# A fused decoder-layer kernel: where the down-weight differences are loaded and formed, and where S1 of the down-projection is summed

## What is computed

```python
h = x + jnp.concatenate([out_a, out_b, out_c], axis=-1) @ lw['w_o']
h = h + memory_attend(rmsnorm(h, lw['norm_mem_g']), mem_k, mem_v, lw)      # ends in o @ lw['w_mo']
u, ffn_buf_new = causal_dwconv(rmsnorm(h, lw['norm_ffn_g']) @ lw['w_up'], ffn_buf, lw['w_ffn_conv'])
ug, uv = split_cols(u, (D_FF, D_FF))
h = h + (jax.nn.silu(ug) * uv) @ lw['w_down']
```

## Time and profile before

| | us |
|---|---|
| runs shown (three) | 1825.99, 1829.52, 1831.13 |
| median | 1829.52 |
| the profiled execution's own time | 1829.62 |
| its span, first to last instruction | 1828.3 |
| PE busy in it | 1754.7 |
| granted TensorE clock, mean | 0.991 |

### The profile page before, as it was taken

One profiled execution on the slowest core, in us unless ns is written; L12 is line 12 of the kernel. 1 busy time (PEld: TensorE's weight loads), 2 busy tenths in 40 slices (PEclk: granted clock), 3 DMA queues, 4 the chain that ended last, 5 costly groups with the idle time before them and its releaser, 6 DMA issues. The chain is left out here.

```text
span 1828.3 us, 27754 instructions
## 1 busy us (share of the span) xinstructions
PE 1754.7 (96%) x10342; PEld 1603.5 (88%) x10342; DVE 1163.1 (64%) x1381; ACT 781.4 (43%) x1489; POOL 725.6 (40%) x617
## 2 busy tenths in 40 slices
PE   6999999989989989999999989999999999999999
PEld 5999999988867778898788879999999999987887
DVE  6236765865665664422537388888888888657964
ACT  5126773325566332312234265444444444443432
POOL 4001211025444250112116027776666666456642
PEclk9999999999989999999999999999999999999999
DMA  6222111233254274133615522222222222499653
GB/s 174 73 60 62 37 36 50 86 97 111 64 155 166 113 279 139 35 115 124 211 42 208 188 66 73 72 72 72 72 72 72 72 72 72 159 321 304 202 181 128
DMA packets 173568, 215.05 MB, mean 118 GB/s; under 512 B 14695, under 2 KB 122600, under 8 KB 171648
## 3 DMA queue, kind: packets, MB, share of 16 engines
q1 hardware_dynamic: 172560, 213.55, 35.9%
q0 software_dynamic: 896, 0.19, 0.1%
q10 hardware_dynamic: 16, 0.00, 0.0%
HBM read 167.11 MB, written 46.60 MB: 117 GB/s over the span
## 5 line engine op out<-in xcount | busy, mean ns | idle before, releaser
L3904 PE MATMUL ffn_banks<-h_parts,up_hi 128*128 128x384 f32 x1920 | 488.7, 335 | 7.9 <-DVE h_parts L4400 4.5
L3904 PEld LDWEIGHTS ffn_banks<-h_parts,up_hi 128*128 128x128 f32 x1920 | 345.7, 188 | 10.0 <-issue 7.8
L3904 PE MATMUL ffn_banks<-h_parts,up_lo 128*128 128x384 f32 x960 | 320.7, 334 | 0.0
L4290 POOL TENSOR_TENSOR up_lo<-up_raw,up_hi 128x512 fp32r<-128x512 f32 x172 | 258.6, 1520 | 130.8 <-ACT up_hi L4059 74.6
L999 PE MATMUL proj_banks<-x_hi,in_w_hi 128*128 128x384 f32 x624 | 212.5, 341 | 0.5 <-DVE x_lo L251 0.5
L999 PE MATMUL proj_banks<-x_hi,in_w_lo 128*128 128x384 f32 x624 | 208.7, 334 | 0.0
L999 PE MATMUL proj_banks<-x_lo,in_w_hi 128*128 128x384 f32 x624 | 208.6, 334 | 0.0
L3904 PEld LDWEIGHTS ffn_banks<-h_parts,up_lo 128*128 128x128 f32 x960 | 180.2, 188 | 0.0
L4340 POOL TENSOR_TENSOR h_parts<-down_cells,h_parts 128x512 fp32r<-128x512 f32 x69 | 105.0, 1525 | 93.3 <-ACT h_parts L4128 93.1
L4015 PE MATMUL ffn_banks<-h_parts,up_hi 128*128 128x512 f32 x352 | 137.8, 391 | 2.3 <-DVE down_cells L4549 2.3
L4018 PE MATMUL ffn_banks<-h_parts,up_lo 128*128 128x512 f32 x352 | 137.7, 391 | 0.0
(11 more groups left out here) (571 smaller groups left out, 3780.2 us busy)
## 6 DMA issues: line engine op xcount, KB each, us to landing
up_raw<-in_w_up SPq DMA_DIRECT2D x44, 512.0 KB, 3.9
up_raw<-ffn_gated_rows SPq DMA_DIRECT2D x44, 320.0 KB, 5.4
ffn_gated_rows<-h SPq DMA_DIRECT2D x22, 576.0 KB, 2.8
in_w_raw<-in_w_in SPq DMA_DIRECT2D x24, 512.0 KB, 3.9
down_cells<-down_sums SPq DMA_DIRECT2D x44, 256.0 KB, 5.0
up_raw<-ffn_gated_rows SPq DMA_DIRECT2D x44, 256.0 KB, 3.9
down_cells<-in_w_down SPq DMA_DIRECT2D x25, 256.0 KB, 5.0
mem_v_and_k_t<-in_w_down SPq DMA_DIRECT2D x6, 1024.0 KB, 6.4
```

The source lines that it names most:

```text
L3904: ins = nc.tensor.matmul(banks[:, bank, 0:TC], wt[:, j, k, :], parts[:, q, x, k, :], start=(fresh and n == 1), stop=(n == last), skip_grou ...
L4290: nc.gpsimd.tensor_tensor(w_lo[:, j], weights.full(j), w_hi[:, j].bitcast(F32), ALU.subtract).then_inc(weights.split[j], 1)
```

## The change

The change has two halves.

In the two projections, pair 5 of the down-weight differences moves from `wo` to `mo`. In `wo` SP issues the weight slices 3 to 7 first, then the residual tiles 0 to 2, then waits for the stored memory and issues the loads of pairs 0 and 1, then the other residual tiles. In `wo` DVE forms pairs 0 to 4 behind the additions n = 4 to 8. In `mo` it forms two pairs ahead of the additions, as before, and the others behind n = 5, 6, 8 and 10.

In the down-projection, S1 is summed two passes ahead: `load_s1` brings both parts, 256 KB each, from n = 9 on, into the cells that S2 and T1 use later, and DVE sums them from n = 11 on (`sum_s1`). Q6's steps then take one load into `a_raw` and one DVE instruction. T2's loads move to n = 18 on and T1's to n = 36 on.

```diff
-WO_SUMS, MO_SUMS = tuple(range(6)), tuple(range(6, NF // 2))
+WO_SUMS, MO_SUMS = tuple(range(5)), tuple(range(5, NF // 2))
...
-        form_at = {-1: steps[0:2], 5: steps[2:4] if residual else steps[2:3], 6: steps[4:5] if residual else steps[3:4],
-                   7: steps[5:6] if residual else steps[4:5]}
+        form_at = dict(zip((4, 5, 6, 7, 8) if residual else (-2, -1, 5, 6, 8, 10), steps))
...
-            if stored_too:
-                sp.wait_ge(stored_too, 32)
-                sp.wait_ge(stored, 16)
-            for k in steps[0:2]:
-                beside.load(sp, k)
+            if not residual:
+                for k in steps[0:2]:
+                    beside.load(sp, k)
             weights.load_rest(sp, w_split)
             for t, rows in enumerate(residual or ()):
                 sp.dma_start(out[:, t, :], rows).then_inc(r_landed[t], 16)
+                if t == together - 1:
+                    sp.wait_ge(stored_too, 32)
+                    sp.wait_ge(stored, 16)
+                    for k in steps[0:2]:
+                        beside.load(sp, k)
...
+                load_a(n, far_pairs if q == Q6 else far if wide(n) else near, i if q in (Q1, Q6, Q5) else STEPS + i)
...
             def load_t2(k):
                 if not k:
                     C.down_sums.wait_stored(sp, STEPS)
-                    for done in (p5, vp, p4, p3):
-                        sp.wait_ge(done, NF)
...
+                sp.wait_ge(s1_formed, k + 1)
                 sp.dma_start(t1_cells[k], sum_of(T1, k)).then_inc(t1_landed[k % T_RING], 16)
 
-            def load_s2(k):
-                sp.dma_start(s2_cells[k], rows_of(k, *near)).then_inc(s2_landed[k], 16)
+            def load_s1(k):
+
+                if not k:
+                    for done in (p5, vp, p4, p3):
+                        sp.wait_ge(done, NF)
+                sp.dma_start(s2_cells[k], rows_of(k, *near)).then_inc(s1_landed[k], 16)
+                sp.wait_ge(a_stored, 16 * (STEPS + k + 1))
+                sp.dma_start(t1_cells[k], rows_of(STEPS + k, *near)).then_inc(s1_landed[k], 16)
...
-                    if n == 6 + k:
+                    if n == 9 + k:
+                        load_s1(k)
+                    if n == 18 + k:
                         load_t2(k)
-                    if n == 27 + k:
+                    if n == 36 + k:
                         load_t1(k)
-                    if n == 16 + k:
-                        load_s2(k)
...
+            def sum_s1(k):
+
+                dve.wait_ge(s1_landed[k], 32)
+                nc.vector.tensor_tensor(s2_cells[k], s2_cells[k], t1_cells[k], ALU.add).then_inc(s1_formed, 1)
+
...
                 if q == Q6:
-                    dve.wait_ge(s2_landed[i], 16)
-                    wait_a_landed(dve, m)
-                    nc.vector.tensor_tensor(s2, s2, raw, ALU.add).then_inc(s2_formed, 1)
-                    wait_a_landed(dve, m + 1)
-                    dve.wait_ge(s2_formed, 2 * i + 1)
-                    nc.vector.tensor_tensor(s2, s2, a_raw[:, (m + 1) % A_RAW, 0:512], ALU.subtract).then_inc(s2_formed, 1)
+                    dve.wait_ge(s1_formed, i + 1)
+                    wait_a_landed(dve, n)
+                    nc.vector.tensor_tensor(s2, s2, raw, ALU.subtract).then_inc(s2_formed, 1)
...
+                if 0 <= n - 11 < STEPS:
+                    sum_s1(n - 11)
```

More of the change, by code:

```diff
@@ L2923, in _ @@
                 low_slice(k)
-            for k in form_at[-1]:
-                beside.form(dve, k)
+            for n in (-2, -1):
+                if n in form_at:
+                    beside.form(dve, form_at[n])
             for n in range(2 * n_tiles):
@@ L2941, in _ @@
                 nc.vector.tensor_tensor(to, to, banks[:, n % 8, :], ALU.add).then_inc(freed, 1)
-                for k in form_at.get(n, ()):
-                    beside.form(dve, k)
+                if n in form_at:
+                    beside.form(dve, form_at[n])
 def query_projection(nc, C, tag, norm, weights, n_tiles, out, inv_norm, beside):
@@ L3580, in ffn @@
         b_landed = [ph.sem(f"f_b_landed{r}") for r in range(B_RAW)]
-        b11_landed, s2_landed = ([ph.sem(f"f_{n}_landed{i}") for i in range(STEPS)] for n in ("b11", "s2"))
+        b11_landed, s1_landed = ([ph.sem(f"f_{n}_landed{i}") for i in range(STEPS)] for n in ("b11", "s1"))
         t1_landed, t2_landed = ([ph.sem(f"f_{n}_landed{r}") for r in range(T_RING)] for n in ("t1", "t2"))
         back_landed = [ph.sem(f"f_back_landed{i}") for i in range(4)]
-        (a_high, a_split_dve, a_split_pool, a_formed, s2_formed, b_high, b_split, fed, down, u_copied,
+        (a_high, a_split_dve, a_split_pool, a_formed, s1_formed, s2_formed, b_high, b_split, fed, down, u_copied,
          taken, added, rows_turned, rows_copied) = (
-            ph.sem(f"f_{n}") for n in ("a_high", "a_split_dve", "a_split_pool", "a_formed", "s2_formed", "b_high", "b_split", "fed", "down", "u_copied", "taken", "added", "rows_turned",
+            ph.sem(f"f_{n}") for n in ("a_high", "a_split_dve", "a_split_pool", "a_formed", "s1_formed", "s2_formed", "b_high", "b_split", "fed", "down", "u_copied", "taken", "added", "rows_turned",
                                        "rows_copied"))
@@ L3642, in wait_a_split, with wait_a_landed @@
                 engine.wait_ge(a_split_dve, sum(not by_pool(i) for i in range(n + 1)))
[L3644 to L3650, removed]
+        def wait_a_landed(engine, n):
+            engine.wait_ge(a_landed[n % A_RAW], 16 * (n // A_RAW + 1))
         def a_cell(n):
[L3653 removed]
+            return s2_cells[n % STEPS] if n // STEPS == Q6 else a_raw[:, n % A_RAW, 0:a_width(n)]
         def b_index(n):
@@ L3741, in rows_of, with load_a, wait_a_free @@
                 return gated_rows[P * (f + 1):P * (f + 2), a:b]
-            def load_a(m, rows, f):
+            def load_a(n, rows, f):
                 sp.wait_ge(a_stored, 16 * (f + 1))
-                sp.dma_start(a_raw[:, m % A_RAW, 0:rows[1] - rows[0]], rows_of(f, *rows)).then_inc(a_landed[m % A_RAW], 16)
+                sp.dma_start(a_raw[:, n % A_RAW, 0:rows[1] - rows[0]], rows_of(f, *rows)).then_inc(a_landed[n % A_RAW], 16)
             near, far, far_pairs = (0, 512), (512, T), (512, 1024)
-            def wait_a_free(m):
-                m -= A_RAW
-                if 2 * STEPS <= m < 4 * STEPS:
-                    sp.wait_ge(s2_formed, m - 2 * STEPS + 1)
-                elif m >= 0:
-                    wait_a_split(sp, m if m < 2 * STEPS else m - STEPS)
+            def wait_a_free(n):
+                n -= A_RAW
+                if n // STEPS == Q6:
+                    sp.wait_ge(s2_formed, n % STEPS + 1)
+                elif n >= 0:
+                    wait_a_split(sp, n)
             def load_step(n):
                 q, i = divmod(n, STEPS)
-                m = a_index(n)
-                wait_a_free(m)
-                if q == Q6:
-                    load_a(m, near, STEPS + i)
-                    wait_a_free(m + 1)
-                    load_a(m + 1, far_pairs, i)
-                else:
-                    load_a(m, far if wide(n) else near, i if q in (Q1, Q5) else STEPS + i)
+                wait_a_free(n)
+                load_a(n, far_pairs if q == Q6 else far if wide(n) else near, i if q in (Q1, Q6, Q5) else STEPS + i)
                 if q in (Q2, Q7, Q4, Q3):
```

11 lines of the change are left out of this document (5 added, 6 removed).

## The result

The kernel before took 1830.76 us (median of 22 runs), the changed one 1833.01 us (median of 22). The ratio is 1.0023, with a 95% interval of 1.0013 to 1.0032: 2.4 to 5.9 us slower, middle 4.2. The forecast was 1829.9 us, in a range of 1822.5 to 1835.0. The time lies in the range, and the middle of the change, 0.23%, is within the 0.3% that the forecast counted as no change (the interval reaches 0.32%). But 4.2 us over the base of 1829.5 is 1833.7, just above the 1826.5 to 1833.0 that the forecast gave its own mechanism, and the sum promised +0.4 us where the runs show about +4. So the terms of that sum have to be gone through again.

A forecast was written before the change was run, and what follows sets the result against it. PE, working 96% of the span, was taken as the bound, so only its waits count. From 1829.6 us, -5.9 + 4.1 + 1.7 - 4.1 + 3.0 + 1.6 = +0.4 gave 1830.0, median 1829.9, range 1822.5 to 1835.0.

The forecast's parts named there:

- its own mechanism: Whole kernel: the summed gains, new waits and clock costs, by itself 1826.5 to 1833.0 us; chance 0.50.
- step 11: Down-projection: S1's extra loads delay n = 14's load, so PE waits for ACT's copies; 3.0 us, bounds 0.5 and 4.5.
- `wo` to n = 13: `wo`: slice 3's wait goes, a new 2.4 us wait for scaled rows comes; gain 5.9 us, bounds 4.5 and 8.2.
- clock behind it: Half-clock stretch after a new wait: 1.7 us behind `mo`'s, 1.6 behind one of those in `wo` and step 11.
- `mo` to n = 13: `mo`: the sixth pair's forming delays the scaling, a new PE wait of 4.1 us; bounds 2.5 and 6.
- step 33: Down-projection: form_a(37) begins earlier, so PE's wait for DVE goes; gain 4.1 us, margin 0.9.
- The lock rule: SBUF port pair: a two-SBUF-input DVE operation and a GpSimd one block each other; form(0) in `wo` taken as 6 us.
- I count one of the two: Of the new waits in `wo` (2.4 us) and step 11 (3.0 us), one brings a half-clock stretch, 1.6 us.
- the forecast's other thought: Step 11: half the extra bytes may fit into slack of the queue ahead, making the wait only 0.5 us.
- the wait stays: Rival, step 33: form_a(37)'s load lands late and DVE is late again; 1834.0 to 1835.8 us, chance 0.18.
- The change does what it says: Rival, `mo` and step 11: neither new wait comes (1820.4 us), or only one (1826.1 or 1824.2); chance 0.22.
- Form(0) is not slowed: Rival, `wo`: the first forming is not slowed and `wo` gives 8.2 us; 1827.6 us, chance 0.10.

The follow-up runs named there:

- wait_first: all3, but in `wo` SP waits for the stored memory ahead of the weight slices, only the pairs' loads staying behind them; 1816.86 us, ratio 0.9940 to the kernel before.
- mo_late: Changed kernel, but the last of `mo`'s six formings stands behind the addition of n = 12 instead of n = 10; 1828.46 us, ratio 0.9995 to the kernel before.
- t1_early: Changed kernel, but T1's eleven loads stand at steps 27 to 37, as in the kernel before, instead of 36 to 46; one execution, 1839.35 us.
- s1_only: Kernel before plus only the down-projection's half of the change (S1 formed two passes ahead), both projections as before; 1829.43 us, ratio 0.9990 to the kernel before.
- s1_later: Changed kernel, but S1's loads (n = 12 to 22) and sums (n = 14 to 24) stand three steps later; 1831.40 us, ratio 1.0008 to the kernel before.
- all3: Changed kernel with three edits: `wo`'s first two pairs formed ahead of its additions, `mo`'s last forming behind n = 12, S1 three steps later; 1818.65 us, again 1818.86.
- wo_ahead: Changed kernel, but `wo` forms its first two pairs ahead of its first addition, the others behind n = 5, 6, 7; 1825.27 us, ratio 0.9981 to the kernel before.

## Why the prediction was right, and where it was not

The mechanisms were the right ones, wait for wait. The sizes were off, four of the six to the side of too much gain, and that the time still fell into the range owes something to luck: those four make 5.1 us together, which would have put the time at 1835.0, the range's upper end, and `mo` and step 11, forecast too dear, took 1.4 of it back. Over all the executions that share a stage's code (five with the changed `wo`, five with `mo`'s wait and seven without, five with S1 at n = 9; of the kernel before's `wo`, step 11 and step 33 there are only two), each term beside its forecast:

| term | forecast, us | measured, us | from |
|---|---|---|---|
| `wo` to n = 13 | -5.9 | -2.9 | 76.30 against 79.18 |
| clock behind it | +1.6, here or in step 11 | +2.3 | 32.26 against 29.94 |
| `mo` to n = 13 | +4.1 | +3.9 | 75.42 against 71.49 |
| clock behind it | +1.7 | +2.4 | 32.33 against 29.90 |
| step 11 | +3.0 | +1.8 | 40.08 against 38.27 |
| step 33 | -4.1 | -3.4 | 29.92 against 33.34 |
| sum | +0.4 | +4.1 | |

The measured sum agrees with the ratio's +4.2. Had only the two profiles been compared, it would have come to +1.2 (the 2.9 of the spans less 2.0 ahead of `wo`, and 0.3 in other untouched stages back): the profile of before happened to have its dearest step 33, that of after its cheapest clock behind `mo`'s wait.

**`wo`, the term that failed.** PE's arrival was forecast for 700.8; it came at 707.14 - 4.35 = 702.79, which is 700.8 when the 2.0 us of the untouched stages are taken off. Slice 3's wait went as worked out, and `wait_first` shows the reason given (the two loads) to be the whole of it. What was wrong is the other side of the wait. Form(0) was put at 6 us and took 7.5, so that its store went at 672.3, 670.3 without those 2.0, instead of 668.6; the two links behind it took 17.6 us instead of 17.4. That makes 1.9, and the wait 4.3 instead of 2.4. (In the forecast's own times there are small slips: 662.8 + 6 is 668.8, and the links were called 8.5 us, from a store's issue to the next load's, but were carried on with 8.8 and 8.6. From load to load the trace of before has 8.9, 8.8 and 8.8.) The 6 us came from one row in which one operation was held up; in the changed kernel all three were, the one with the broadcast operand the longest. The row just ahead of that one, in the same timeline of the kernel before, shows a second operation held:

```profile
655.25 2.88 DVE L2731 TENSOR_TENSOR mem_v_and_k_t<-mem_v_and_k_t 128x512 f32<-128x512 f32 x1
```

With the third, free one, that form(0) took 6.9 us, and the whole of it would have been a better basis than one row. The lock rule that the prediction drew on (the Trainium skill, SBUF — State Buffer, "SBUF: two separate sides") is borne out: the runs show 2.6 us with POOL at rest and 7.5 beside it. Taken at its word, for all three operations, it would have given the right size: three POOL tiles of 2.4 to 2.9 us one after the other, 8.0 in all.

The other 1.1 us between -5.9 and -2.9 is not an error of the chain but of the pair of executions compared. Two of the five with the changed `wo` ran with a clock of 0.83 from 632 to 642 us (`mo_late`, `t1_early`), and so did `s1_only`, whose `wo` is that of before, so the change did not bring it; and the execution of before that was costed was 0.5 above the mean of the two.

**The clock.** "I count one of the two" was the wrong choice for `wo`. Of 11 waits of 3.5 to 6.7 us ahead of an n = 13, in `wo` and `mo` together, all 11 had a stretch of half clock that reached past their end: the part behind took 31.25 to 32.76 us. Of the 11 passages without a wait and the two with one of 0.7 to 0.8 none had (29.90 to 29.94). Step 33's 2.3 us wait cost 4.25 once and 2.59 once; behind the waits of 0.4 and 1.0 us in step 11 of the changed kernel the granted clock stayed at 1.00.

**`mo`.** The load was forecast for 1021.5, the form for 1027.9, the end of the scaling for 1033.5; the rows say 1021.50, 1027.92, 1033.40. PE was forecast to be ready at 1029.4 and was at 1029.94, which is most of why the wait is 3.6 and not 4.1. This is the case in which the chain had near rows of its own kind and nothing else beside it.

**Step 11.** The place and the engine were right, the size was too large. The forecast let the extra 1.31 MB delay the load of n = 14 byte for byte, by 3.3; it came 2.06 later in the two profiled executions, 2.4 over all. Less the margin of 0.25 that is 1.8 in the pair, whose stage grew by 1.96, and 2.2 over all, where it grew by 1.8. That would fit the forecast's other thought, that some of the bytes find slack in the queue; but taking six of the loads away again brought 0.73 each, more than their bytes, so slack alone does not explain both. The timelines of SP say a little more. Of the 2.06, 1.84 are there already when SP issues the load (25.45 us after the first matmul before, 27.29 after), with some 0.45 us for each issue; from issue to ACT's start it is 10.7 and 10.9. In `s1_later` the load goes at 25.3 and needs only 8.8. So five loads more cost SP's time, and six fewer shortened both. Why the queue did not charge the bytes of the five stays open.

**Step 33.** form_a(37) was forecast 1.0 us ahead of PE's first matmul of the step (1684.4 to 1685.41) and came 1.07 ahead. SP got there a little later than forecast, and the load took 9.2 us to DVE's start instead of 9.9. The term is -3.4 and not -4.1, because the 4.1 was that one execution's price with the half clock in it. The rival "the wait stays" did not come; but in the ten executions with this down-projection form_a(37) began between 1.40 us ahead of PE's first matmul and 0.22 behind it, and at 0.22 (in `all3`, once) PE lost 0.26. The forecast's margin of 0.9 was of the right size. The rival's picture, one more load of T1 directly ahead of the five `h_kept` loads, does not fit the queue: the kernel before issues a load of T1 in the same place (1678.44, the first `h_kept` at 1678.92), and `t1_early`, with ten of T1's loads issued by then, has the same room as the changed kernel.

**The other rivals.** "The change does what it says" had its say only in part: neither wait was absent, since `mo`'s followed from the order and step 11's from a margin of 0.25 us. "Form(0) is not slowed" is refuted in the changed kernel, and true in `wo_ahead`, where it is formed elsewhere.

## What to carry to other kernels

A chain that alternates a store, a load and an operation ends late by as much as its first link does: begin it where DVE and POOL both rest, check whether the queue is free for its first store (10.6 us in a full one, 3.9 in an empty one), and put no step that waits for a load ahead of the step on the same engine that TensorE waits for. Moving one forming behind the scaling gave 5 us and beginning the chain early 8 (3.5 under before instead of 4.2 over), without a byte or an instruction less. Where an edit's terms are a few microseconds of both signs, take each from all executions that have the stage in common, and count the half clock with a wait as part of its price (it came with all 11 waits of 3.5 us and more here).

## What the runs showed of the hardware

DVE's subtraction with the broadcast operand is held by POOL's as the plain ones are: 3.31 us beside POOL, 1.22 alone (668.99 and 656.04 above). One more case, in the kernel with the three edits, where POOL's tile and DVE's second operation meet by chance, on POOL and on DVE:

```profile
676.57 2.52 POOL L2909 TENSOR_TENSOR wo_act_lo<-mixT,wo_act_hi 128x1024 fp32r<-128x1024 f32 x1 [6.46 <-ACT wo_act_hi L2857]
...
676.88 2.77 DVE L2733 TENSOR_TENSOR mem_v_and_k_t<-mem_v_and_k_t 128x512 f32<-128x512 f32 x1
```

POOL ends at 679.09 and DVE 0.55 later, near the 0.69 that the operation takes alone, which fits an operation that waited out the whole tile and then ran.
